# Half of the query projection and half of the output layer between the attention's steps on TensorE, with the query norm applied to the scores

## The reference

```python
hk = rms_norm(h, g_kv_norm);  kv = (hk @ w_kv).reshape(N, T, 2, 4, 64)
k, v = rms_norm(kv[:, :, 0], g_k_norm), kv[:, :, 1]
hq = rms_norm(h, g_attn_norm)
q = rms_norm((hq @ w_q).reshape(N, T, 4, 4, 64), g_q_norm)      # norm over each head's 64
s = q k^T * 64**-0.5 + rel_bias, masked to a window of 128      # prompt: 2 blocks of 128
p = exp(s - m) / (sum(exp(s - m)) + exp(sink - m));  o = p v    # m = max(s, sink)
h = h + o @ w_o
h = h + moe_swiglu(rms_norm(h, g_moe_norm))
```

## Time and profile before

| | us |
|---|---|
| median of three runs | 1561.8 |
| lowest, highest | 1558.99, 1562.72 |
| the profiled execution, its own time | 1560.62 |
| its span | 1558.8 |
| busy over the span: PE, DVE, ACT, POOL | 1520.7, 1218.9, 969.2, 116.4 |
| mean granted TensorE clock | 0.986 |

### The profile page before, as it was taken

The page is one execution under the profiler, slowest core; times in us unless marked ns, Lnnn a source line. Parts: engine busy times, 40 slices in busy tenths (PEclk is TensorE's granted clock), DMA queues, the critical chain, the costliest instruction groups (busy, mean ns, idle before and its releaser), DMA issues.

```text
span 1558.8 us, 22061 instructions
## 1 busy us (share of the span) xinstructions
PE 1520.7 (98%) x7891; PEld 1284.1 (82%) x7891; DVE 1218.9 (78%) x1237; ACT 969.2 (62%) x1072; POOL 116.4 (7%) x99
## 2 busy tenths in 40 slices
PE   8998999999989989999999999999999999999998
PEld 6986999999975968888888888888888888888776
DVE  6995545446696458888888889889889889889886
ACT  6554443344564247677777677777777677767764
POOL 1001011011320010000000000000000000000000
PEclk9999999999998979999999999999999999999999
DMA  8930345444531549989989998998998998998992
GB/s 348 175 128 27 108 162 177 144 156 150 187 123 50 193 177 372 367 310 404 398 321 385 395 356 349 401 381 321 412 373 314 422 370 309 423 377 300 414 366 106
DMA packets 66259, 438.48 MB, mean 281 GB/s; under 512 B 8069, under 2 KB 10373, under 8 KB 15648
## 3 DMA queue, kind: packets, MB, share of 16 engines
q1 hardware_dynamic: 57312, 412.38, 67.6%
q0 software_dynamic: 5552, 19.36, 5.1%
q10 hardware_dynamic: 3344, 6.05, 1.1%
HBM read 423.73 MB, written 15.03 MB: 281 GB/s over the span
## 4 chain that ended last, share of the span: by engine, by line
PE 92%; DVE 3%; DMA 2%; ACT 1%; issue 1%; POOL 1%; SPq 0%; ACTq 0%; DVEq 0%; POOLq 0%
PE bank L354 27%; PE bank L356 27%; PE bank L355 27%; PE bank L402 3%; PE bank L779 2%; DMA land<-in_w_expert 1%; PE bank L376 1%; DMA land<-in_w_dense 1%; PE bank L628 0%; PE bank L711 0%; PE bank L602 0%; PE bank L657 0%; PE bank L717 0%; PE bank L580 0%; PE bank L617 0%
## 5 line engine op out<-in xcount | busy, mean ns | idle before, releaser
L1474 DVE TENSOR_TENSOR w_lo<-land,w_hi 128x2048 fp32r<-128x2048 f32 x224 | 504.3, 2289 | 78.2 <-ACT w_hi L1078 76.3
L1078 ACT CAST w_hi<-land 128x2048 fp32r<-128x2048 f32 x224 | 418.5, 1913 | 6.4 <-issue 3.5
L354 PE MATMUL bank<-w_hi,xe_hi 128*128 128x512 f32 x896 | 364.8, 407 | 1.6 <-DVE xe_lo L1560 1.0
L356 PE MATMUL bank<-w_hi,xe_lo 128*128 128x512 f32 x896 | 354.3, 395 | 0.0
L355 PE MATMUL bank<-w_lo,xe_hi 128*128 128x512 f32 x896 | 353.0, 394 | 0.0
L1573 DVE TENSOR_TENSOR d_lo<-land,d_hi 128x2048 fp32r<-128x2048 f32 x112 | 256.8, 2292 | 44.6 <-ACT d_hi L1081 43.7
L1081 ACT CAST d_hi<-land 128x2048 fp32r<-128x2048 f32 x112 | 213.9, 1911 | 122.3 <-PE bank L356 119.1
L356 PEld LDWEIGHTS bank<-w_hi,xe_lo 128*128 128x128 f32 x896 | 168.4, 188 | 39.4
L354 PEld LDWEIGHTS bank<-w_hi,xe_hi 128*128 128x128 f32 x896 | 169.0, 189 | 36.2 <-DVE xe_lo L1560 1.2
L355 PEld LDWEIGHTS bank<-w_lo,xe_hi 128*128 128x128 f32 x896 | 169.1, 189 | 34.1
L354 PE MATMUL bank<-d_hi,heT_hi 128*128 128x512 f32 x448 | 177.3, 396 | 1.1 <-DVE heT_lo L1605 1.1
(11 more groups left out here) (264 smaller groups left out, 2088.4 us busy)
## 6 DMA issues: line engine op xcount, KB each, us to landing
land<-in_w_expert SPq DMA_DIRECT2D x336, 1024.0 KB, 6.4
land<-in_w_dense SPq DMA_DIRECT2D x54, 1024.0 KB, 4.9
rel_rows<-rb POOLq DMA_DIRECT2D x1, 3072.0 KB, 36.1
bias<-rel_rows ACTq DMA_DIRECT2D x4, 512.0 KB, 4.8
y_rows<-zero_rows POOLq DMA_DIRECT2D x3, 512.0 KB, 10.8
X<-in_x SPq DMA_DIRECT2D x4, 288.0 KB, 5.7
out_y<-X SPq DMA_DIRECT2D x2, 576.0 KB, 2.8
Us<-in_state POOLq DMA_DIRECT2D x1, 1088.0 KB, 9.5
```

The costliest lines, as they stand in the source:

```text
L354: pe.matmul(out, w[0], x[0], start=start, stop=False)
L356: return pe.matmul(out, w[1], x[0], start=False, stop=stop)
L1078: act.copy(w_hi[n % RING][:], land[(DENSE + u) % LAND][:]).then_inc(hi_done, 1)
L1474: dve.tensor_tensor(w_lo[n % RING][:], land[slot][:], w_hi[n % RING][:].bitcast(F32), ALU.subtract).then_inc(split, 1)
```

## The change

- The roles of H and G change places: keys and values read G, queries read H. So the half of the queries that comes later can still read H when G's memory has become the bias and score tiles.
- PE projects query tiles 0 to 3 ahead of the scores, 4, 5 and 6 after `scores(1)`, and 7 within step 1. The fillers go.
- The queries are no longer normalised. ACT squares them straight out of the bank and copies them with the gain. PE takes the means per token in `query_means` (the squares are the stationary operand; three matmuls per tile). ACT takes roots for four tiles at a time (`query_root`), DVE the reciprocals (`query_scales`). The token's own scale cancels but for eps, which is folded in as `eps_tok` and `eps_col`. The scale then multiplies the scores: `soft_args` has one operation for each of four heads, (bank x scale) + bias, where it had one or two adds. For the samples POOL multiplies the scale into `QZ`, and the roots and reciprocals of those scales are made in steps 2 and 3.
- The samples' step moves from fifth to sixth place, behind (2, 0). The samples' output uses bank 7 in place of 6, step 2's probabilities lie in `SS`.
- The output layer's tiles are cut in two along k. The first halves (heads of kv 0 and 1, `output_half`, banks 2 and 3) are issued after the samples' output is split: 0 to 4 between the last steps, 5 to 7 after them. DVE adds each to `X` (`add_half`). The second halves take the old place. The last three weight units are split at fixed places within the steps instead of all at its ends.

The diff, cut to its core:

```diff
-        STEPS = [(0, 0), (0, 1), (1, 0), (1, 1), None, (2, 0), (2, 1), (3, 0), (3, 1)]
+        STEPS = [(0, 0), (0, 1), (1, 0), (1, 1), (2, 0), None, (2, 1), (3, 0), (3, 1)]
+        SAMPLES = STEPS.index(None)
...
+            def query_means(t):
+
+                ng, g = divmod(t, GR)
+                out, at = MEANS[ng]
+                pe.wait_ge(kq_sq, 2 + t + 1)
+                if t == 0:
+                    pe.wait_ge(rt_ready, 1)
+                for b in range(2):
+                    pe.matmul(out[:, at + 2 * GR * b + 2 * g:at + 2 * GR * b + 2 * g + 2], sq[:, t % 2, P * b:P * b + P],
+                              c("mean_head")[:, 0:P:HD], start=True, stop=True)
+                a = at + 4 * GR + NS * g
+                pe.matmul(out[:, a:a + NS], c("mean_head"), sq[:, t % 2, SEQ:T], start=True, stop=True).then_inc(q_ms, 1)
+
+            def query(t, out):
+
                 n = U_Q + t // 2
                 pe.wait_ge(split, n + 1)
-                pe.wait_ge(kq_copied, t + 1 if t < 2 else max(2, t - 1))
-                if t == 2:
-                    pe.wait_ge(v_ready, 1)
                 for k in range(KT_D):
                     if t == 0:
                         wait_h(4, k)
-                    last = mm3(bank[t % 4][:, 0:T], wblock(n, KT_D * (t % 2) + k), G(k),
-                               k == 0, k == KT_D - 1)
+                    last = mm3(out[:, 0:T], wblock(n, KT_D * (t % 2) + k), H(k), k == 0, k == KT_D - 1)
                 last.then_inc(kq_done, 1)
                 if t % 2:
                     pe.wait_ge(kq_done, 2 + t + 1)
                     pe.sem_inc(used, 1)
+
+            for t in range(GR):
+                if t < 2:
+                    pe.wait_ge(kq_copied, t + 1)
+                if t == 2:
+                    pe.wait_ge(v_ready, 1)
+                query(t, bank[t])
                 if t >= 1:
-                    head_mean(2 + t - 1)
-            head_mean(2 + KT_D - 1)
+                    query_means(t - 1)
+            query_means(GR - 1)
...
+                if STEPS[s] == (2, 1):
+                    pe.wait_ge(q_root, 4)
+                    pe.wait_ge(qs_sum, 2)
...
-                    pe.wait_ge(kq_sd, 2 + KT_D)
-                    for _ in range(FILL):
-
-                        pe.matmul(bank[4][:, 0:256], ident, con[:, 0:256], start=True, stop=True)
+                    pe.wait_ge(kq_sd, 2)
...
+                if s == 0:
+                    pe.wait_ge(q_root, 2)
+                    pe.wait_ge(qs_sum, 1)
...
+            def output_half(d):
+
+                n = U_O + d // 2
+                pe.wait_ge(split, n + 1)
+                if d == 0:
+                    pe.wait_ge(o_ready, OUT_STEPS.index(SAMPLES) + 1)
+                if d < 2:
+                    pe.wait_ge(s_ready, [SAMPLES, SAMPLES + 2][d] + 1)
+                else:
+                    pe.wait_ge(x_half, d - 1)
+                for k in range(GR):
+                    last = mm3(bank[3 - d % 2][:, 0:T], wblock(n, KT_D * (d % 2) + k), H(k), k == 0, k == GR - 1)
+                last.then_inc(wo_half, 1)
+
+            pe.wait_ge(kq_copied, 2 + GR)
+            pe.wait_ge(kq_ready, 2)
             scores(0)
             scores(1)
+            query(4, bank[1])
+            pe.wait_ge(kq_sd, 2)
+            query(5, bank[5])
+            pe.wait_ge(kq_copied, 2 + 5)
+            query_means(4)
+            query(6, bank[1])
             for s in range(len(STEPS)):
-                if s + 2 < len(STEPS):
+                if s == 2:
+                    attend(1)
+                    pe.wait_ge(kq_copied, 2 + KT_D)
+                    query_means(7)
+                if s + 2 < len(STEPS) and s + 2 != SAMPLES:
                     scores(s + 2)
-                if s >= 1:
+                if s >= 1 and s != 2:
                     attend(s - 1)
+                if s > SAMPLES + 1:
+                    output_half(2 * (s - SAMPLES) - 3)
                 turn_probs(s)
+                if s > SAMPLES:
+                    output_half(2 * (s - SAMPLES) - 2)
+                if s == 1:
+                    pe.wait_ge(kq_copied, 2 + 7)
+                    query_means(5)
+                    query_means(6)
+                    query(7, bank[1])
+                if s + 2 == SAMPLES:
+                    scores(SAMPLES)
             attend(len(STEPS) - 1)
+            for d in range(5, KT_D):
+                output_half(d)
...
+                elif d >= 2:
+                    pe.wait_ge(x_half, KT_D if d == 2 else KT_D - 1)
+                else:
+                    pe.wait_ge(s_ready, len(STEPS))
+                for k in range(GR, KT_D):
+                    last = mm3(bank[d % 4][:, 0:T], wblock(n, KT_D * (d % 2) + k), H(k), k == GR, k == KT_D - 1)
...
+            def query_copy(t):
+
+                act.wait_ge(kq_done, 2 + t + 1)
+                if t < 2:
+                    act.wait_ge(kq_ms, t + 1)
+                else:
+                    act.wait_ge(q_ms, t - 1)
+                src = bank[[0, 1, 2, 3, 1, 5, 1, 1][t]][:, 0:T]
+                act.activation(sq[:, t % 2, :], src, ACT.Square).then_inc(kq_sq, 1)
+                act.activation(Q[:, t, :], src, ACT.Identity, scale=g_q8[:, 0:1]).then_inc(kq_copied, 1)
+
+            def query_root(ng):
+
+                out, at = MEANS[ng]
+                act.wait_ge(q_ms, GR * ng + GR)
+                for b in range(2):
+                    a = at + 2 * GR * b
+                    act.activation(q_scale[:, b, ng, :], out[:, a:a + 2 * GR], ACT.Sqrt,
+                                   bias=eps_tok[:, b:b + 1]).then_inc(q_root, 1)
+
+            for t in range(GR):
+                query_copy(t)
+                hi_to(U_Q + t // 2 + RING)
 
             act.wait_ge(rb_stored, 16)
             for n in range(2):
                 act.dma_start(bias[:, n], toeplitz(GR * n, GR, P, P - 1, 2 * P)).then_inc(in_bias[n], 16)
-            head_root(2 + KT_D - 1)
+            act.wait_ge(eps_ready, 2)
+            query_root(0)
...
-            hi_to(DENSE)
+            hi_to(U_O + 2)
             exps(0)
+            query_copy(4)
             for s in range(len(STEPS)):
                 if s + 1 < len(STEPS):
                     exps(s + 1)
+                if s == 0:
+                    query_copy(5)
+                    query_copy(6)
...
+                if s == 1:
+                    query_copy(7)
+                if s == 2:
+                    query_root(1)
+                    act.wait_ge(qs_sum, 2)
+                    act.activation(q_scale_s[:], q_scale_s[:], ACT.Sqrt).then_inc(qs_root, 1)
+                if s == 3:
+                    hi_to(U_O + 3)
+                if s == 5:
+                    hi_to(DENSE)
...
-            for t in range(KT_D - 1):
-                head_norm(2 + t, Q[:, t, :], g_q8[:])
-                if t < KT_D - 2:
-                    lo_to(U_Q + t // 2 + RING)
-
+
+            dve.wait_ge(rt_ready, 1)
+            seq(dve.reciprocal(eps_tok[:], r_tok[:, 0:2]))
+            dve.scalar_tensor_tensor(out=eps_tok[:], in0=eps_tok[:], scalar=EPS, in1=eps_tok[:],
+                                     op0=ALU.mult, op1=ALU.mult).then_inc(eps_ready, 1)
+            dve.scalar_tensor_tensor(out=eps_col[:], in0=sd[:, SEQ:T], scalar=EPS, in1=sd[:, SEQ:T],
+                                     op0=ALU.mult, op1=ALU.mult).then_inc(eps_ready, 1)
+            lo_to(U_O + 1)
+            dve.wait_ge(eps_ready, 2)
+
+            def query_scales(ng):
+
+                out, at = MEANS[ng]
+                dve.wait_ge(q_root, 2 * ng + 2)
+                seq(dve.reciprocal(q_scale[:, :, ng, :], q_scale[:, :, ng, :]))
+                a = at + 4 * GR
+                dve.tensor_tensor(q_scale_s[:, GR * ng:GR * ng + GR, :],
+                                  out[:, a:a + GR * NS].rearrange("p (g t) -> p g t", g=GR),
+                                  eps_col[:].unsqueeze(1).to_broadcast([P, GR, NS]), ALU.add).then_inc(qs_sum, 1)
+
+            query_scales(0)
...
-                for h in range(b + 1):
-                    gs = GR // (b + 1)
-                    last = dve.tensor_tensor(probs(s)[:, gs * h:gs * h + gs, :],
-                                             bank[2 * (s % 2) + h][:, :].rearrange("p (g s) -> p g s", g=gs),
-                                             bias[:, n % 2, gs * h:gs * h + gs, 2 * P - w:2 * P], ALU.add)
+                ng, i = divmod(n, 2)
+                for g in range(GR):
+                    h, a = divmod(g * w, 512)
+                    last = dve.scalar_tensor_tensor(out=probs(s)[:, g, :], in0=bank[2 * (s % 2) + h][:, a:a + w],
+                                                    scalar=q_scale[:, b, ng, 2 * g + i:2 * g + i + 1],
+                                                    in1=bias[:, n % 2, g, 2 * P - w:2 * P], op0=ALU.mult, op1=ALU.add)
...
+            def add_half(d):
+
+                dve.wait_ge(wo_half, d + 1)
```

(32 more changed lines are left out.)

70 lines of the change are left out of this document (32 added, 38 removed).

## The result

The changed kernel takes 1572.6 us (median of four runs, 1571.7 to 1573.5) against 1561.0 for the kernel before (four runs, 1559.0 to 1562.7) on the same chip: a ratio of 1.0075, 95% interval 1.0057 to 1.0092. It is slower by more than the 0.3% that a measurement can tell. The forecast was 1564, with 1571 as its upper end. The profiled execution took 1573.5 with a span of 1571.6, against 1560.6 and 1558.8.

A forecast was written before the change was run, and what follows sets the result against it. PE was taken as busy outside the attention, which lost 19.6 of 58.0 us to waits, fillers and half clock. Layout -2.4 plus clock 4.6 gave +2.2: 1562.8 profiled, 1564 as median, range 1556 to 1571.

The forecast's parts named there:

- Clock: Attention and first output halves: half clock after the longer waits adds 0 to 7 us, 4.6 taken.
- (c): PE's wait before the samples' transposes, 4.2 us: normalise(5) stands behind o_lo(3) and soft_args(6).
- The layout's -2.4: Instructions laid out engine by engine without half clock: output ends at 540.8 against 543.2, 2.4 us sooner.
- Start: Four query tiles instead of eight before the scores: scores(0) starts at 431.4 instead of 448.40, 17.0 us sooner.
- (a): PE's wait before step 3's transposes, 5.3 us: query tile 7, table load and root hold up ACT and DVE.
- (b): PE's wait before the samples' scores, 2.6 us: root, reciprocal and POOL's products must come first.
- Output: Second output halves after the attention: 23.4 us in the layout, off 36.8 for whole tiles.
- Rival 5: DVE bounds the second output halves if a tile pair needs over 7.0 us; at 9 us 1570; chance 0.05.
- Rival 6: Each ACT table switch has a drain, 1.4 us longer at both switches of (a): 1566.8; chance 0.04.
- Rival 2: The clock stays up through dense matmuls inside the attention: 1559.4, or 1558 with cheap scalar operations; chance 0.18.
- Rival 3: Only some 6 of the attention's 16.6 us of waits remain: 1549 at full clock, 1553 with some drop; chance 0.10.
- Rival 4: Half clock from (c) through the first half tiles, shorter after (a): +7, scalar operations +1.4, 1567.8; chance 0.19.

The follow-up runs named there:

- fill_more: Changed kernel with query tile 4 between scores(0) and scores(1) and 23 filler matmuls, 4 of them where PE has no wait: 1565.4 us, ratio 1.0029.
- before_filled: Kernel before with 11 filler matmuls, 5 before step 2's transposes and 6 ahead of the samples' PV: 1563.95 us, ratio 1.0013.
- root_first: Changed kernel with roots ahead of step 2's copy, normalise(3) and query_scales(1) before soft_args(4), tile 4 between scores(0) and scores(1): 1567.1 us, ratio 1.0040.

## Why the prediction was wrong

The step that failed is **Clock**: 4.6 us taken, within "0 to 7". When I lay the instructions after each other again, with the three measured stretches at 0.50, the last half tile ends at 529.5, 13.1 us later than at full clock; the profile has 530.4. This is an estimate; `fill_more` measures about 12 for the same. The 13.1 are 2.9, 3.9 and 7.7 for each stretch alone (together less, since waits absorb some). Behind (c) I priced 4.6, and it was 7.7 by this estimate, because the stretch went on through the samples' second PV half, T6, the first half tile and PV6. The other two I had at nothing: that at 435 because four dense query tiles stood just ahead of it, that from 465.9 because I priced only what follows (c). At both places stood what I had read off ahead of a fall, waits or matmuls of few rows or columns, and had not looked for in the new order. That this is the cause isn't shown: the first stretch came in some executions and not in others. The forecast's profiled 1562.8 becomes 1573.5 by 8.5 of clock (13.1 for 4.6), 1.3 ahead of the queries, 1.4 in the experts' stage, and -0.5 of small terms.

The layout's -2.4 also compared unlike things, a changed kernel without half clock and the kernel before with 20.5 us of it. By the prediction's own 3.0 us for that, the kernel before would reach the routing at 540.2 at full clock, and the changed one at 540.8. So there was no gain to protect, only a clock loss that could grow.

Two smaller slips nearly cancel. The listed waits add up to 16.9, not 16.6. And the samples' scores, 4.8 us in the sum of work at full clock, ran partly at 0.50 (463.42 to 466.83 in the earlier trace rows); with the clock up they take 4.2 in `fill_more`.

- *Start*: 16.5 us from first query to scores for 16.0. Right. That the queries begin at 416.76 instead of 415.45 needs no effect of the change: they begin at 417.08 in `before_filled`, and between 416.8 and 418.0 in the others. Ahead of them the profile before has 3.4 us at 0.50, the changed kernel and `before_filled` 10.2 each.
- *DVE*: 1.12 and 1.66 us a step, cheaper than the 1.3 and 1.85 taken, inside both bounds. POOL's products 1.98 (1.8 taken). Reciprocal 1.75 as said.
- *Waits (a), (b), (c)*: 5.3, 2.6 and 4.2 forecast; 4.06, 1.90 and 3.43 measured, each behind the engine named. Right in place and cause. Half clock ahead of the first two used up part of them: with the clock up, `fill_more` leaves 4.95 and 2.70 for them, fillers and rest together. The third was 0.8 too long by itself.
- *Output*: 24.0 for 23.4, cut as in the earlier trace rows. Rival 5 never came up.
- *Table loads*: 1.28 each as in the earlier trace rows, 1.42 for the first with what stands around it, and only one on the path where I had counted both. Rival 6 out.
- *Rival 2*, the clock stays up: out by itself. `fill_more` has the clock up through the attention, and at 1565.4, or some 1563.7 less its 1.7 of fillers, it is still 4 us over the rival's 1559.4. In its profile a stretch at 0.50 reaches 5.6 us into the experts' stage, which is 2.8 us longer than before's.
- *Rival 3*, the waits go: out, though `root_first` shows that 3 us of them could.
- *Rival 4*, half clock from (c) through the first half tiles: this is what happened, and more; its +7 should have been +12.
- *Fixed*: the routing (24.8 us for 24.7 from the last output matmul's end) was. The experts' stage takes 991.2 to 992.3 in the nine profiles where the clock is up again at its first matmul, and 992.8 to 994.7 in the five where a stretch at 0.50 reaches into it (after: 578.56 to 581.98). I had taken it as fixed.

What is left open is why the norm-on-scores form costs 7 us beyond its layout, apart from its going along with more half clock, and what part the samples' later place has in it. Open too is what makes the clock fall at one place in one execution and not in the next, and where the some 3 us lie by which the changed kernel stays over the kernel before in the medians when its attention runs at full clock.

## What to carry to other kernels

Where one pours dense work out of a long block in between narrow work, price TensorE's clock as a term of its own: mark every wait and every run of few-row or few-column matmuls in the new order, and take up to half the length of the stretch that may follow at 0.50 (here 0.3 of it, where waits took up a part). Here it was five times the layout's gain. Compare like with like: lay out both kernels at full clock, then add the clock to both. Before blaming a chain of waits, fill the waits with matmuls that nobody reads: if the kernel gets faster, the wait's price was the clock. And time the parts of a combined change alone; here the one that saved the most instructions cost 15 us with its order of steps, one move gave back 4, and the other nothing that can be told from noise.

## What the runs showed of the hardware

- A stretch at 0.50 with PE busy for 6.83 of 6.83 us (435.20 to 442.03): half clock isn't only for an engine that waits.
- The same instructions with the same history in the program ran at either level in two executions (2.68 and 1.89 us for the same eight score matmuls). The Trainium skill ("TensorE: Matmul & The Clock Gate", Part 1) says that the same kernel starts with a different number of matmuls at the low clock from run to run. These two traces show such a difference in the middle of a kernel. Here it was worth 3.1 us, so one profile can be that far off for this alone.
- Matmuls that nobody reads paid for themselves: in `fill_more` 4 of 23 cost their full 0.43 us, and the kernel, with tile 4 moved too, was 7 us faster.
- Half clock that reaches over the experts' first matmuls (0.43 us apart for 0.23) goes with 1 to 3 us more of their stage.
